# Two hybrid transformer layers on one core: Gram banks masked whole and laid beside the first inverse level, rows over heads in one pass, the output projection by halves of its contraction

## Reference

```python
# forgetting attention, first layer; F[t, h] is the running sum of log sigmoid(f)
s = einsum('bhqd,bhkd->bhqk', q, k) * scale + Fq[..., None] - F[:, :, None, :]
s = where(q_pos[:, None] >= k_pos[None, :], s, -inf); p = softmax(s)
...
# RWKV-7 recurrence, second layer: kk is k normalized over each head's 64 channels
S = S * w_t + (S a_t) b_t^T + v_t k_t^T;  y_t = S r_t        # per head, per token
y = (y - mean(y)) * rsqrt(var(y) + eps)                      # over each head
...
# gated delta rule: q, k normalized over each head, o normalized over each head
o = o * rsqrt(mean(o * o) + eps) * norm_w * silu(z)
y = concatenate([y_a, y_b]);  x = x + y @ w_out
x = x + (silu(h @ w_gate) * (h @ w_up)) @ w_down
```

## Time and profile before

| what | value |
|---|---|
| median of 3 runs | 2990.61 us (2983.4 to 2995.9) |
| the profiled execution's own time | 2997.93 us |
| its span | 2996.2 us |
| mean granted TensorE clock, as a share of 2.4 GHz | 0.984 |
| PE busy | 2923.0 us (98%) |
| DVE busy | 1604.5 us (54%) |
| ACT busy | 1166.9 us (39%) |
| DMA, mean over the span | 167 GB/s |

### The profile page before, as it was taken

The page is one execution under the profiler, slowest core; times in us unless marked ns, Lnnn a source line. Parts: engine busy times, 40 slices in busy tenths (PEclk is TensorE's granted clock), DMA queues, the critical chain, the costliest instruction groups (busy, mean ns, idle before and its releaser), DMA issues.

```text
span 2996.2 us, 42957 instructions
## 1 busy us (share of the span) xinstructions
PE 2923.0 (98%) x18850; PEld 2518.7 (84%) x18850; DVE 1604.5 (54%) x1332; ACT 1166.9 (39%) x956; POOL 53.0 (2%) x119
## 2 busy tenths in 40 slices
PE   8999999999999999999998999899799999999998
PEld 7999788888888888888888999898678888888887
DVE  5757554445554545454465767764455444544445
ACT  4354443343443333433343434223244343333333
POOL 0000000000000000020011000000000000000000
PEclk9999999999999999999999999898799999999999
DMA  6556556666555555555554545100145555555554
GB/s 214 166 159 183 153 160 192 194 187 194 183 192 187 192 185 194 184 189 191 195 197 160 171 141 159 39 4 31 57 155 189 189 189 189 191 187 186 193 196 168
DMA packets 257288, 501.00 MB, mean 167 GB/s; under 512 B 12176, under 2 KB 17627, under 8 KB 256763
## 3 DMA queue, kind: packets, MB, share of 16 engines
q1 hardware_dynamic: 257147, 498.87, 51.8%
HBM read 496.74 MB, written 2.10 MB: 166 GB/s over the span
## 4 chain that ended last, share of the span: by engine, by line
PE 95%; DVE 3%; ACT 1%; DMA 0%; issue 0%; SPq 0%; DVEq 0%; ACTq 0%
PE psum L658 23%; PE psum L660 23%; PE psum L659 23%; PE psum L643 5%; PE psum L645 5%; PE psum L646 5%; PE psum L1070 3%; PE psum L956 1%; DVE weight_lo L1801 1%; PE psum L709 1%; PE psum L950 0%; PE psum L604 0%; DMA weight_raw<-in_w_in 0%; ACT weight_hi L1339 0%; PE psum L1034 0%; PE psum L872 0%
## 5 line engine op out<-in xcount | busy, mean ns | idle before, releaser
L1801 DVE TENSOR_TENSOR weight_lo<-weight_raw,weight_hi 128x2048 fp32r<-128x2048 f32 x460 | 1054.2, 2292 | 1129.1 <-ACT weight_hi L1339 1128.7
L1339 ACT ACTIVATE weight_hi<-weight_raw 128x2048 fp32r<-128x2048 f32 x460 | 881.2, 1916 | 1505.5 <-PE psum L660 1204.4
L658 PE MATMUL psum<-weight_hi,h_both 128*128 128x512 f32 x1856 | 725.1, 391 | 0.0
L660 PE MATMUL psum<-weight_hi,h_both 128*128 128x512 f32 x1856 | 722.6, 389 | 0.0
L659 PE MATMUL psum<-weight_lo,h_both 128*128 128x512 f32 x1856 | 722.1, 389 | 0.0
L643 PE MATMUL psum<-h_both,weight_hi 128*128 128x256 f32 x1408 | 404.8, 288 | 16.3 <-DVE weight_lo L1801 16.3
L660 PEld LDWEIGHTS psum<-weight_hi,h_both 128*128 128x128 f32 x1856 | 348.3, 188 | 72.8
L659 PEld LDWEIGHTS psum<-weight_lo,h_both 128*128 128x128 f32 x1856 | 348.5, 188 | 71.4
L658 PEld LDWEIGHTS psum<-weight_hi,h_both 128*128 128x128 f32 x1856 | 348.4, 188 | 71.3
L645 PE MATMUL psum<-h_both,weight_lo 128*128 128x256 f32 x1408 | 401.4, 285 | 0.0
L646 PE MATMUL psum<-h_both,weight_hi 128*128 128x256 f32 x1408 | 401.3, 285 | 0.0
(11 more groups left out here) (511 smaller groups left out, 2310.4 us busy)
## 6 DMA issues: line engine op xcount, KB each, us to landing
weight_raw<-in_w_in SPq DMA_DIRECT2D x144, 1024.0 KB, 5.5
weight_raw<-in_w_ffn_in SPq DMA_DIRECT2D x88, 1024.0 KB, 5.0
weight_raw<-in_w_ffn_out SPq DMA_DIRECT2D x44, 1024.0 KB, 5.1
weight_raw<-in_ffn_w_gate SPq DMA_DIRECT2D x44, 1024.0 KB, 5.2
weight_raw<-in_ffn_w_up SPq DMA_DIRECT2D x44, 1024.0 KB, 5.1
weight_raw<-in_ffn_w_down SPq DMA_DIRECT2D x44, 1024.0 KB, 5.1
weight_raw<-in_w_out SPq DMA_DIRECT2D x32, 1024.0 KB, 5.1
weight_raw<-in_w_branch_rnn SPq DMA_DIRECT2D x8, 1024.0 KB, 5.0
```

The source lines that it names most:

```text
L658: mm(acc[:, t, :], xh[:, c], wh[:, k, :], start=(start and k == 0), stop=False, skip_group_check=True)
L660: last = mm(acc[:, t, :], xl[:, c], wh[:, k, :], start=False, stop=(stop and k == CK - 1), skip_group_check=True)
L1339: A(hi[j % g.hi][:], raw[j % g.ring][:], ACT.Copy).then_inc(hi_ready, 1)
L1801: V.tensor_tensor(lo[r][:], raw[r][:], hi[j % g.hi][:].bitcast(F32), ALU.subtract).then_inc(lo_ready, 1)
```

## The change

1. **Rows in one pass.** A row is now kept as two: the part rounded to fp32r, and what is left of it (`split_rows`, `inverse_rows`, `low_rows`). The rows fill 32 partitions instead of 16 (partitions 32 to 63 for the norms), `head_rows_r` is an fp32r copy of `sel` spread over 64 partitions by three DMAs, and one fp32r matmul adds both parts. The forget rows and the causal mask of the attention go the same way. The decay rows and the matmul of gd_eg stay f32.
2. **Gram banks.** DVE multiplies a whole bank by its masks in one instruction (128 x 512 into `rw_gram`) and writes the low part of X and of its transpose over an identity with a predicated copy. The identities are written by POOL beforehand (two copies of 128 x 2048, `eyes_made`). The last copy of tokens (`v_tokens2`, second half) moves from DVE to ACT. PE's pairs come in the order b, b, x, k, k for each half; the last pairs and the value products go in between the first level of the inverse, and one set of decay rows moves into level k = 1.
3. **Output projection by halves.** The first two strips are computed together: chunks 0 and 1 of both strips, then chunks 2 and 3 of both; so are the last two. `outputs` is split in three.

```diff
@@ wo2 and PE
+        HALVES = ((0, 0), (0, 1), (1, 0), (1, 1), (0, 2), (0, 3), (1, 2), (1, 3))
-                   lambda i: [sl(w_o2, k, i * 1024 + s * CN) for s in range(2) for k in range(4)])
+                   lambda i: [sl(w_o2, k, i * 1024 + s * CN) for s, k in HALVES], {5: 0, 7: 1})
+            def halves_product(before):
+                def turned(q):
+                    pe.wait_ge(strips_out, wo2.sbase + q + 1)
+                    turn_x(q, 2 + q % 2, X)
+                rhs = wo2.strips[0][1]
+                for i in range(2):
+                    for j, (s, c) in enumerate(HALVES):
+                        if i == 0 and before[j]:
+                            before[j]()
+                        if i == 0 and s == 0:
+                            pe.wait_ge(y2_parts, c + 1)
+                        if i and c == 0:
+                            pe.wait_ge(n_u, 12 + s + 1)
+                        product_tokens(wo2, i, j, token_pair(2 + s), lambda k: rhs(CK * c + k), c == 0, c == 3)
+                        if i and j == 0:
+                            turned(1)
+                        if j == 6:
+                            turned(2 * i)
+                return lambda: turned(3)
-            last_turn = out_product(wo2, y2_parts, 0, 3, (None, state_product, outputs))
+            last_turn = halves_product((None, state_product, outputs, output_sums, output_scales, None, None, None))
@@ rows over heads and scores
-            def over_heads(b0, rows, n0=0, n1=NT):
+            def over_heads(b0, rows, n0=0, n1=NT, heads=sel_r[UP, :]):
-                    ... sel[:, n * P:(n + 1) * P], rows[:],
+                    ... heads[:, n * P:(n + 1) * P], rows,
-                    mm(dst, sel[:, h * P:(h + 1) * P], row_sums[:, 0:n], ...)
-                    last = mm(s[:, t * P + o:t * P + n], ident[:], causal[:], ...)
+                    mm(dst, sel_r[0:4 * H, h * P:(h + 1) * P], f_rows_r[:, 0:n], ...)
+                    last = mm(s[:, t * P + o:t * P + n], ident_r[:], causal_r[:], ...)
+            def split_rows(rows, r, p):
+                settle(V.tensor_copy(r[p, :], rows[p, :]))
+                return V.scalar_tensor_tensor(r[p, :], r[p, :].bitcast(F32), low_rows[p, :], rows[p, :], ALU.mult, ALU.add)
+            def inverse_rows(rows, r):
+                settle(V.reciprocal(rows[UP, :], rows[UP, :]))
+                return split_rows(rows, r, UP)
@@ Gram
+        GRAMS = [(cp, kind, g) for cp in range(2) for kind, g in (("b", 0), ("b", 1), ("x", 0), ("k", 0), ("k", 1))]
+        GRAM_BANKS = (0, 2, 4, 6, 0, 2, 4, 6, 2, 6)
+            gp.wait_ge(*at_step("bonus_kept"))
+            gp.wait_ge(chunks_used, in2.end)
+            for x in (x_r, xt_r):
+                last = gp.tensor_copy(x[:], bcc(chunk_eye, 32))
+            last.then_inc(step("eyes_made"), 1)
```

More of the change, by code:

```diff
@@ L36, with __init__ @@
     ring, hi = 4, 2
-    def __init__(self, before, strips, bodies, sources):
+    def __init__(self, before, strips, bodies, sources, ends=None):
         self.strips, self.bodies, self.sources = strips, bodies, sources
@@ L468, in _ @@
             sp.dma_start(w_pl[:], a["w_pool"][0].rearrange("g (t p) d -> p g t d", p=P)).then_inc(mw_landed, 16)
-            for i in range(1, in1.bodies):
+            load(in1, 1)
+            sp.wait_ge(mix_tables, 2)
+            for r in range(2 * H, 64, 2 * H):
+                sp.dma_start(sel[r:r + 2 * H, :], sel[0:2 * H, :]).then_inc(S("head_rows_copied"), 16)
+            for i in range(2, in1.bodies):
                 load(in1, i)
@@ new lines, in gram_products @@
+            def gram_products(i):
+                cp, kind, g = GRAMS[i]
+                if i < 4:
+                    pe.wait_ge(S("rw_kv_tok_out" if i == 2 else "rw_ab_tok_out"), (4, 4, 3, 5)[i])
+                else:
+                    earlier = max(k for k in range(i) if GRAM_BANKS[k] == GRAM_BANKS[i])
+                    pe.wait_ge(S("rw_gram_out"), 2 * earlier + 2)
+                l = {"b": bt_f, "k": Kw, "x": None}[kind]
+                for n in range(4 * g, 4 * g + 4) if l is not None else range(8):
+                    for c in range(2):
+                        tc = slice((2 * cp + c) * CH, (2 * cp + c + 1) * CH)
+                        for half in range(2):
+                            r = slice(64 * half, 64 * half + 64)
+                            o = bank(GRAM_BANKS[i] + half)[64 * c:64 * c + 64, :]
+                            if l is None:
+                                last = mm(o[:, n * 64:(n + 1) * 64], at_f[r, n, tc], bt_f[r, n, tc], start=(n == 0), stop=True,
+                                          skip_group_check=True)
+                            else:
+                                last = mm(o[:, (n % 4) * P:(n % 4 + 1) * P].rearrange("p (m t) -> p m t", m=2), l[r, n, tc],
+                                          AR[r, :, n, tc], start=(n % 4 == 0), stop=True, skip_group_check=True)
+                last.then_inc(S("rw_gram"), 2)
@@ L1090, in inverse_x, with decay_rows @@
                 of_chunks(bank(5 + 2 * (b % 2)), lambda r, u: z_r[r, u, :], lambda r, u: xt_r[r, u, :], 8, 8 * b).then_inc(S("inv_x"), 1)
+            def decay_rows(half):
+                pe.wait_ge(S("gd_fall"), 2 * half)
+                over_heads(2, row_sums[:], 4 * half, 4 * half + 4,
+                           sel_r[0:2 * H, :].bitcast(F32)).then_inc(step(f"gd_g_rows{half}"), 1)
+            for i in range(8):
+                gram_products(i)
             for k in range(5):
+                if k == 0:
+                    pe.wait_ge(S("rw_gram_out"), 10)
                 inverse_z(k, 0)
+                if k == 0:
+                    gram_products(8)
                 inverse_z(k, 1)
+                if k == 0:
+                    gram_products(9)
                 inverse_x(k, 0)
@@ L1814, in split @@
                             continue
-                        if j == d and not first:
-                            f(i - 1, g.ns - 1)
+                        if not first and j + g.per - 1 - d in g.ends:
+                            f(i - 1, g.ends[j + g.per - 1 - d])
                         elif j > d and j - 1 - d in g.ends:
@@ L1894, in _ @@
             to_slot(0, 0)
-            dve.wait_ge(par_landed, 16 * (sum(len(g) for g in groups) + 8))
-            V.tensor_copy(wf2[:].rearrange("p k (m r) -> p (k m) r", r=2),
-                          wf[:].rearrange("p k m -> p (k m)").unsqueeze(2).to_broadcast([P, KT * H, 2])).then_inc(step("wf_spread"), 1)
+            dve.wait_ge(par_landed, 16 * (sum(len(g) for g in groups) + 10))
+            for m in range(2):
+                last = V.tensor_copy(wf2[:, :, 2 * H * m:2 * H * (m + 1)].rearrange("p k (h r) -> p k h r", r=2),
+                                     wf[:].unsqueeze(3).to_broadcast([P, KT, H, 2]))
+            last.then_inc(step("wf_spread"), 1)
             chunks(in1, 0, 5, 6)
@@ L2321, in _ @@
             dve.wait_ge(*at_step("kk_root"))
-            V.reciprocal(kk_rows[:], kk_rows[:]).then_inc(step("kk_rows"), 1)
+            inverse_rows(kk_rows, kk_rows_r).then_inc(step("kk_rows"), 1)
             chunks(in2, 3, 5, 6)
```

295 lines of the change are left out of this document (171 added, 124 removed).

## The result

| kernel | median (range), us | runs | ratio to before, 95% |
|---|---|---|---|
| before, on the chip of this comparison | 2993.26 (2983.4 to 2997.43) | 4 | |
| changed | 2953.18 (2950.81 to 2961.71) | 4 | 0.9876 (0.9843 to 0.9909) |

The account below looks back on a forecast made before the run. PE, busy 98% of the span, was taken as the bound. Gains of 9 + 6.3 + 11.7 + 7 + 16.7 = 50.7 us off the median of 2990.6 gave 2940 us, range 2925 to 2964.

Parts of the forecast that it names:

- Scores: Attention scores: four f32 matmuls per head become fp32r, 1.68 us to 0.48; gain 9 us over 8 heads.
- The lower bound of 4: Attention scores: if the three narrow fp32r matmuls gain nothing, 8 x 0.5 = 4 us is left.
- kk: Rows of kk: 8 matmuls go from 4.1 to 1.0 us, and the clock stays up behind; gain 6.3, at least 3.1.
- the two terms: Attention scores and rows of kk, up to the last rows: gains of 9 and 6.3 us.
- Gram stage: Last rows to end of inverse level 0: 50.2 us before; gain 11.7, or 7.5 if the identities are late.
- The identities: POOL's two copies ahead of DVE's masks: 4.4 us, no wait; rival of late identities or masks, chance 0.12.
- Transposes: 64 turns behind the last rows: 8.3 us at full clock; rival 16.6 at low clock, time 2948, chance 0.03.
- Delta stage: Two sets of rows give 5.5 us, the split costs 0.8, the clock gives 2.3; gain 7, bounds 4 and 11.
- output projection: Second output projection by halves: waits shrink, 5.6 + 11.1 = 16.7 us gained; 10 if late, 20 if the wait vanishes.
- The wait behind the rows: Output projection: y_out, its rounding and its rest are not hidden, some 3.2 us with the rows' end.
- the low clock after the wait: Output projection: the low clock behind the wait on y_out's parts was left as it was, with no gain counted.
- the sum is taken off the median: Last step: the 50.7 us, summed on the profiled 2997.9, is taken off the median 2990.6, giving 2939.9.

Follow-up runs that it names:

- m5_rows_first: Changed kernel with each head's score matmuls reordered to both rows, both masks, both q and k products; a head takes 1.21 us, single time 2947.23 us.
- m1_scores_grouped: Changed kernel with each head's score matmuls ordered rows, mask, rows, mask, then both q and k products; a head takes 1.51 us, single time 2953.44 us.
- u3_rows_only: Changed kernel with the old output projection order and old Gram part put back, leaving only one-pass rows; 2977.14 us, ratio 0.9943 to before.
- m4_eyes_twice: Changed kernel with both identities written twice on GpSimd; last rows to end of inverse level 0 41.5 us, single time 2960.11 us.
- i1_out_delta: Changed kernel with delta work one chunk earlier in the output projection and two DVE orders moved in the delta stage; 2935.43 us, ratio 0.9805 to before.
- b2_gate_split: `i1_out_delta` plus rows-first scores, reordered delta stage end, gate product cut in two and the gate2 product behind the aqk masks; 2925.23 us, ratio 0.9778 to before.
- m3_rows_x4: Changed kernel with every fp32r matmul of rows over heads done four times; single time 2968.99 us.

## Why the prediction was right, point by point

- **In the main right:** 47.0 us between the profiled executions where the sum had 50.7, each of the three parts with the sign and roughly the size forecast, 2953 in the range of 2925 to 2964.
- **Scores, the mis-sized term: 5.4 instead of 9.** "One pass each at 0.12" was the distance of like matmuls. The measured distances are 0.17 to 0.31 (0.90 per head for 0.48), because 32 rows follow 128 and back (`m5_rows_first` against `m1_scores_grouped`). I had named the change of type as the thing to allow for, and that was the wrong one. A smaller error: for the second mask I took 0.32, and the timeline of before has 0.25 (327.09 to the weight product at 327.34), so the four cost 1.61, not 1.68. The lower bound of 4 held.
- **kk: right in kind.** 1.22 us for 8 matmuls and the clock at 1.00 behind them. Of the 15.3 us of the two terms 10.3 came. Following the same weight product through both traces shows where: 1.0 ahead of the scores, 5.6 at them (the weight product behind each head is 0.03 shorter too), 5.5 at kk, less 1.3 at the first product of the second layer, for which PE waits longer than before, and less 0.5 between there and kk, where a new wait of 0.5 us for a `weight_lo` stands. Before, then after:

```profile
1599.54 0.55 PE L643 MATMUL psum<-h_both,weight_hi 128*128 128x256 f32 x1 [9.91 <-DVE weight_lo L1801]
```

```profile
1594.22 0.55 PE L681 MATMUL psum<-h_both,weight_hi 128*128 128x256 f32 x1 [11.26 <-DVE weight_lo L1899]
```

All twelve profiles of the experiments have 10.9 to 11.6 there and the 0.5 behind it, `u3_rows_only` too, so the loss comes with the one-pass rows and is no chance of one execution; what in them lengthens the wait is open. The 0.8 missing at kk were counted twice: the low clock began some 1.4 us before the rows' end, so part of it was already in their 4.1.
- **Gram stage: 10.9 against 11.7**, by partly other numbers. The predicated copy was priced at 0.3; its starts stand 0.24 apart for 128 elements and 0.6 for 256. POOL took 1.90 per copy for 2.2. The end of level 0 followed its last rows by 39.3, where "some 38" was said.
- **The identities:** late from 1.7 us on, and then one to one (`m4_eyes_twice`). In time, as the one-input row said.
- **Transposes:** from 1905 to 1909 us PE does nothing but turns, the clock there is 1.00, and eight of them take 1.04, as in the row below. The rule of the Trainium skill ("TensorE: Matmul & The Clock Gate", Part 4, PE-mode transpose), by which they would not run at the full rate, disagrees with this trace too.

```profile
1905.58 1.04 PE L1096 MATMUL psum<-ident,log_decay 128*128 128x128 f32 x8
```

- **Delta stage 7.7 against 7, output projection 16.8 against 16.7.** In the delta stage the terms held one by one: 5.7 for the two sets of rows where 5.5 was said, a wait of 4.08 instead of 3.13 where 0.8 more was said, and the rest, 2.9, for the clock where 2.3 was said. The wait behind the rows, 3.2 forecast, is 3.26. I had let "the low clock after the wait" stand as it was. It is there (0.55), and it was worth removing, as `i1_out_delta` shows.
- **The step that failed is the last one: "the sum is taken off the median".** 7.3 of the 13 us between 2940 and 2953 come of it; 3.6 are the sum's own error (50.7 for 47.1), and 2.4 are that the profiled execution of the changed kernel lies that much below its median. The profiled execution of before was 7.3 above its median, and I took off the same 50.7, as if a typical execution had the same low-clock patches to give back. Executions of one kernel differ by such patches: the two profiles of the changed kernel differ by 9.9 us, most of it one patch. The gain of a patch can be had only where it was. That the typical execution of before lacked some of its patches is argued; only one was profiled.

## What to carry to other kernels

What a matmul with few rows costs depends on what stands around it as much as on its passes: put tiles with the same number of rows next to each other, and keep a stretch of few rows short (cutting one by full products may do as well; `b2_gate_split` suggests it and does not show it). When a wait on another engine falls right behind such a stretch, look for what that engine did in the idle time just before; here the two orders of DVE moved by a place shortened the delta stage by 9.5 us, where the change itself gave 7.7. When a sum is made from one profile, ask which of its clock patches a typical execution has before setting it against a median.

## What was not expected of the hardware

- A start of a 32-row fp32r matmul beside 128-row ones costs 0.25 to 0.31 us, against 0.12 from like to like the earlier trace rows and 0.15 among eight of 32 rows (8 in 1.22).
- The gate product (16 f32 matmuls of 128 rows and 16 of 32, 10 us in one piece) halved the clock for 10 to 17 us in five of twelve executions and left it alone in the others. Cut in two pieces of 5 us with a chunk between them, five executions lay within 2.4 us and the profiled one has no such patch; whether the cut did it is not shown, since one kernel with the product in one piece had five executions within 1.2 us as well.
- 32 fp32r matmuls of 32 rows in one stretch halved the clock once (kk in `m3_rows_x4`, 5.17 us with the fall in it) and left it at 1.00 once (l2 in the same execution, 4.06 us).
- COPY_PREDICATED of 128x128 runs 427 ns, of 128x256 749 ns; a whole-bank mask of 128x512 takes 693 ns. By their starts (0.24, 0.60 and 0.61 to 0.63 apart) the predicated copy is the dearer one per element, and it takes the place of two (a mask, and the addition of the identity).
